# Second product of the opening feed-forwards as seven products of halves, with their late side panels on GpSimd

## The chip, the cores and the metric

One core of a Trainium2 chip runs the kernel. The metric is the device time of one execution in microseconds. The kernel before takes 2571.94 us (median of three runs, 2569.3 to 2572.46).

## The reference, cut to what matters

The kernel computes a first transformer block (mixers and a mixture of experts) and then a second one of two layers, all in fp32, for 256 tokens of width 1024. The change touches the first feed-forward of each of the two layers, and the modulation vector that is computed beside it:

```python
def swiglu(h, w_in, w_out):
    gate, up = jnp.split(h @ w_in, 2, axis=-1)
    return (jax.nn.silu(gate) * up) @ w_out
...
for l in range(DEPTH_2):
    mod = cond @ w_ada[l] + b_ada[l]
    sh1, sc1, g1, sh2, sc2, g2, sh3, sc3, g3 = jnp.split(mod, N_MOD, axis=-1)
    h = modulate_2(rms_norm_2(x), sh1, sc1)
    x = x + 0.5 * g1[:, None, :] * swiglu(h, w_ff1_in[l], w_ff1_out[l])
    ...
    h = modulate_2(rms_norm_2(x), sh3, sc3)
    x = x + 0.5 * g3[:, None, :] * swiglu(h, w_ff2_in[l], w_ff2_out[l])
```

The inner width of a feed-forward is 2816, which is 22 blocks of 128. The product in question is the one with `w_out`: 1024 x 2816 by 2816 x 256 tokens.

## The kernel before, in words

Activations lie transposed, features on the 128 partitions, 256 tokens along the free axis. The output of a feed-forward's second product is made in eight chunks of 128 features. Three stages matter: `first_layer`, `between` and `last`. `LayerIn` is the opening feed-forward of a layer with the projection behind it and runs in `first_layer` and in `between`; `LayerOut` is the closing feed-forward and runs in `between` and in `last`.

In both, the first product of the feed-forward is done in ten groups (`Groups`), each as seven products of halves (Strassen's scheme) instead of eight, with VectorE making the sums and differences of halves, and ScalarE taking results out of PSUM. A group takes TensorE about 12.5 us.

The second product differs. `LayerOut` uses `Down` (line 2022): two chunks of features form a pair, a pair and the two halves of the tokens form a 2x2 product of halves over 11 blocks, and each of the four pairs takes seven products of 11 matmuls with 128 columns. For each pair VectorE makes four differences of weights of 128x1408 (lines 2133 to 2149); once it makes five sums of halves of the hidden activations (line 2151), and for each pair it joins the products (`dve_join`, line 2162), updates the residual `xT` and scales the new chunk for what follows. `order` (line 2047) is the order of the products on TensorE, `made` (line 2049) the order in which VectorE finishes its results; each product waits for its count. `LayerIn` instead does plain products (`pe_add`, line 1796): 8 chunks of 22 matmuls with 256 columns, and `dve_add` behind each.

Beside the opening feed-forward runs the side work, the modulation vector `cond @ w_ada`. Its weights come in 28 side panels of 128x2048 through four side slots. `side_panel` (line 2622, VectorE) multiplies each half of a panel (1024 columns) by a per-partition factor and adds it to one of three totals; four panels make one tile of modulation values. Then TensorE sums the tile over the partitions (`tile_sum`, line 2308), ScalarE copies the row out, TensorE turns it (`turn`, line 2318) and VectorE adds the bias (`tile_add`, line 2616). Panels 0 to 15 lie beside the groups, panels 16 to 27 beside the chunks of the second product (`beside_chunk`, line 2227). SyncE loads the next panels when slots are free (`side_loads`, line 2272), in one queue with the feed-forward's weights and the weights of the projection that follows; `small` and `consts` are loaded once the last tile is summed, since `consts` holds the totals.

Behind the second product TensorE runs the leading product of the projection (`pe_lead`), which needs every scaled chunk and then one bank that the turns use. GpSimd does nothing in this stage; it clears two tiles later (line 2799).

Of the kernel before, what the change touches and what calls it, by code (L numbers as in the profile page):

```python
# [7 lines left out]
P = 128  # L8
D = 1024
KD = D // P  # L10
T = 256
# [7 lines left out]
KF = D_FF // P  # L19
# [1579 lines left out]
SIDE = 4  # L1599
GROUPS = 10  # L1600
# [421 lines left out]
class Down:  # L2022
# [3 lines left out]
    def __init__(self, st, c, d, l, ring, hid, room, scratch, tail, groups):  # L2026
        self.c, self.d, self.groups = c, d, groups
        self.made, self.product, self.kept = (st.sem(f"down{l}_{k}") for k in ("made", "product", "kept"))
# [11 lines left out]
        self.z = d.ps[5]  # L2040
# [38 lines left out]
    def pe_product(self, pe, p, i):  # L2079
# [22 lines left out]
        if p == 6:  # L2102
            self.wait_made(pe, f"t2_{i}")
            self.wait_made(pe, "s2")
            out, left, right = self.z[:, P:2 * P], self.t2, lambda k: self.s2[:, k]
# [7 lines left out]
        if p == 4:  # L2113
            self.wait_made(pe, f"t4_{i}")
            pe.wait_ge(self.kept, i + 1)
# [17 lines left out]
    def dve_weights(self, ve, i):  # L2133
# [28 lines left out]
    def dve_join(self, ve, i):  # L2162
        z, w, a, c = self.z, self.bank(i), self.a[i % 2], self.c
        ve.wait_ge(self.kept, i + 1)
        ve.wait_ge(self.product, self.count[3, i])
        if i:
            ve.wait_ge(self.d.x_updated, KD + 2 * i)
# [15 lines left out]
    def dve_odd(self, ve, i, gain):  # L2183
        d, q = self.d, 2 * i + 1
        ve.wait_ge(d.chunk_done, KD + 2 * i + 2)
# [5 lines left out]
class LayerIn:  # L2191
# [8 lines left out]
    def __init__(self, st, c, l, ring, buffers, ff_here, ps, xT, hT, cond, vec, small, mod, gain, proj, mix, consts, cst,  # L2200
                 tables, b, final_g, vec_src, small_src, consts_src, w_ada, w_ff, w_in, lead, begun, room, group_sems):
# [16 lines left out]
        groups = Groups(c, d, group_sems, l, hid, room, mix.rearrange("p k n -> p (k n)"))  # L2218
        x_sq = proj[:, 14:14 + KD]
# [111 lines left out]
        def tensor(pe, beside_values, beside_last):  # L2331
# [44 lines left out]
            d.pe_lead(pe, d.slots[0].rearrange("p (b n) -> p b n", n=P), 1, {3: lambda pe: d.pe_sum_folded(pe, 1)})\  # L2376
# [112 lines left out]
        def scalar(sc, beside_last):  # L2489
# [145 lines left out]

        def first_gain(ve):
# [4 lines left out]
        def vector(ve):  # L2641
# [1597 lines left out]
```

## Time and profile before

| | |
|---|---|
| median of three runs | 2571.94 us |
| the profiled execution's own time | 2572.24 us |
| its span, first to last instruction | 2570.5 us |
| TensorE busy (matmuls) | 2185.2 us, 85% |
| VectorE busy | 1118.7 us, 44% |
| ScalarE busy | 469.6 us, 18% |
| GpSimd busy | 6.1 us |
| mean granted TensorE clock | 0.933 |

PE is TensorE, PEld its weight loads, DVE is VectorE, ACT is ScalarE, POOL is GpSimd, SP is SyncE. A fp32 matmul stands in the trace as two records. A timeline row begins with the start and the length in us of a run of like instructions; the starts of successive rows show the pace, while the length of a row contains the pipeline's tail.

### The profile page before, as it was taken

How to read it: one execution, taken by the hardware profiler on the slowest of the kernel's cores; microseconds unless marked ns; L12 is line 12 of the kernel's file. 1: busy time of each engine (PE TensorE's matmuls, PEld its weight loads, DVE VectorE, ACT ScalarE, POOL GpSimd, SP SyncE). 2: the span in 40 equal slices, each digit the busy share in tenths (PEclk: the TensorE clock that was granted, in tenths of full speed). 3: DMA queues.
4: the chain of work that ended last, by engine and by line, in shares of the span. 5: the costliest groups of instructions: out<-in, count | busy, mean ns of one | idle time of the engine just before them, and what ended most of it. 6: DMA issues, size and time to landing. Idle time of an engine off the chain costs nothing. (4 is left out here: it accounts for less than half of the span.)

```text
span 2570.5 us, 30945 instructions
## 1 busy us (share of the span) xinstructions
PE 2185.2 (85%) x12430; PEld 1523.6 (59%) x12430; DVE 1118.7 (44%) x1941; ACT 469.6 (18%) x1049; POOL 6.1 (0%) x11
## 2 busy tenths in 40 slices
PE   8999986565666665655899999999999999999998
PEld 5786832111111211111588887788998888778898
DVE  5753631000000100000486557567668754756554
ACT  3204010000000000000222044322212203442220
POOL 0000000000000000000000000000000000000000
PEclk9999989878878788888999999999999999999999
DMA  9653799999999999999977632067447763115430
GB/s 391 231 223 122 282 411 416 428 428 428 428 428 427 428 428 428 428 427 427 420 305 290 256 106 84 2 274 299 165 197 289 278 258 141 49 49 215 173 153 17
DMA packets 75207, 721.61 MB, mean 281 GB/s; under 512 B 8656, under 2 KB 11728, under 8 KB 13520
## 3 DMA queue, kind: packets, MB, share of 16 engines
q1 hardware_dynamic: 75088, 719.95, 68.3%
q8 instruction: 83, 1.36, 0.2%
q14 instruction: 36, 0.29, 0.0%
HBM read 718.87 MB, written 1.05 MB: 280 GB/s over the span
## 5 line engine op out<-in xcount | busy, mean ns | idle before, releaser
L1315 PE MATMUL bank<-pool,moe_x_cur 128*32 128x512 f32 x1776 | 259.8, 722 | 143.1 <-DMA pool<-in_w_expert 143.1
L1315 PEld LDWEIGHTS bank<-pool,moe_x_cur 128*32 128x32 f32 x1776 | 54.2, 122 | 336.2 <-DMA pool<-in_w_expert 229.7
L1340 PE MATMUL bank<-pool,moe_hidT 128*32 128x512 f32 x864 | 148.0, 821 | 70.3 <-DMA pool<-in_w_expert 62.5
L1497 DVE TENSOR_TENSOR moe_hid<-bank,moe_silu 128x512 f32<-128x512 f32 x16 | 11.1, 691 | 443.4 <-ACT moe_silu L1457 443.4
L1809 PE MATMUL bank<-trunk_proj,pool 128*128 128x256 f32 x704 | 155.5, 380 | 0.0
L1887 PE MATMUL bank<-pool 128*128 128x256 f32 x640 | 152.1, 381 | 0.0
L1887 PE MATMUL bank<-spare,trunk_mix 128*128 128x256 f32 x640 | 146.7, 382 | 3.6 <-ACT first_layer_sq L1946 3.6
L2364 PE MATMUL bank<-pool 128*128 128x256 f32 x672 | 148.3, 380 | 0.0
L1887 PE MATMUL bank<-pool,trunk_mix 128*128 128x256 f32 x640 | 145.9, 381 | 0.0
L1809 PEld LDWEIGHTS bank<-trunk_proj,pool 128*128 128x128 f32 x704 | 132.5, 190 | 19.8 <-issue 2.5
L2364 PEld LDWEIGHTS bank<-pool 128*128 128x128 f32 x672 | 127.2, 190 | 21.2 <-issue 4.2
L1887 PEld LDWEIGHTS bank<-spare,trunk_mix 128*128 128x128 f32 x640 | 122.6, 192 | 20.9 <-issue 4.0
L1887 PEld LDWEIGHTS bank<-pool,trunk_mix 128*128 128x128 f32 x640 | 122.6, 192 | 17.0
L1340 PEld LDWEIGHTS bank<-pool,moe_hidT 128*32 128x32 f32 x864 | 28.2, 132 | 174.1 <-DMA pool<-in_w_expert 105.5
L1887 PEld LDWEIGHTS bank<-pool 128*128 128x128 f32 x640 | 117.6, 190 | 17.2 <-issue 3.3
L787 PE MATMUL bank<-pool 128*128 128x256 f32 x576 | 126.8, 379 | 1.0 <-PEq L3160 1.0
L1501 DVE COPY moe_y<-bank 128x512 f32<-128x512 f32 x16 | 11.1, 691 | 267.1 <-PE bank L1340 250.2
L787 PEld LDWEIGHTS bank<-pool 128*128 128x128 f32 x576 | 109.2, 190 | 19.1 <-issue 4.7
L1457 ACT ACTIVATE moe_silu<-bank 128x512 f32<-128x512 f32 x16 | 9.6, 597 | 564.6 <-PE bank L1315 564.6
L1354 PE MATMUL bank<-moe_place,moe_y 128*128 (+1 forms) x256 | 73.8, 439 | 43.8 <-DVE xT L1510 26.3
L1354 PEld LDWEIGHTS bank<-moe_place,moe_y 128*128 128x128 f32 x256 | 52.6, 216 | 78.7 <-DVE xT L1510 33.6
L1510 DVE SCALAR_TENSOR_TENSOR xT<-bank,first_mod,xT 128x256 f32<-128x256 f32 x128 | 53.2, 477 | 78.0 <-PE bank L1354 78.0
(689 smaller groups left out, 3202.8 us busy)
## 6 DMA issues: line engine op xcount, KB each, us to landing
pool<-in_w_expert SPq DMA_DIRECT2D x165, 2048.0 KB, 35.6
pool<-in_w_ff SPq DMA_DIRECT2D x132, 1024.0 KB, 6.9
pool<-in_w_ada SPq DMA_DIRECT2D x66, 1024.0 KB, 8.9
moe_more<-in_w_expert SPq DMA_DIRECT2D x23, 2048.0 KB, 36.1
pool<-in_w_in SPq DMA_DIRECT2D x40, 1024.0 KB, 4.9
pool<-in_w_mod SPq DMA_DIRECT2D x24, 1024.0 KB, 7.7
pool<-in_w_out SPq DMA_DIRECT2D x10, 1024.0 KB, 9.9
pool<-in_small SPq DMA_DIRECT2D x2, 2560.0 KB, 9.3
```

What stands on the lines that cost most here:

```text
L787: mm = pe.matmul(ps[p % 3][:, j * T:(j + 1) * T], w[:, j * KD + k], h[:, k], start=k == 0, stop=k == KD - 1)
L1315: mm = pe.matmul(ps[b][quarter[g], :], x_cur[:, u], w[:, b, g], start=u == 0, stop=u == up_panels - 1)
L1340: mm = pe.matmul(ps[2 + b][quarter[g], :], hidT[:, s, g], w[:, g, b], start=s == 0, stop=s == down_panels - 1)
L1354: mm = pe.matmul(ps[at][:, (j % 2) * T:(j % 2 + 1) * T], y[:, k * P:(k + 1) * P], place_of[:, e], start=True, stop=True)
L1457: sc.activation(silu, ps[0], ACT.Silu).then_inc(silu_done, 1)
L1497: ve.tensor_tensor(hid, ps[1], silu, MUL).then_inc(hid_done, 1)
L1501: ve.tensor_copy(y[:, 512:D], ps[3]).then_inc(y_high, 1)
L1510: m = ve.scalar_tensor_tensor(xT[:, k], ps[at][:, (j % 2) * T:(j % 2 + 1) * T], gate[:, k:k + 1], xT[:, k], MUL, ADD)
L1809: mm = pe.matmul(self.ps[3 + q % 2][:, 0:T], w, x[:, k], start=k == 0, stop=k == nk - 1)
L1887: mm = pe.matmul(bank, left[:, k], right[:, k], start=start and k == 0, stop=k == 3, skip_group_check=True)
L2364: mm = pe.matmul(ps[n % 3][:, j * T:(j + 1) * T], slot[:, j * KD + k], hT[:, k], start=k == 0, stop=k == KD - 1)
```

## The change

The second product of the opening feed-forwards goes through `Down` too. `Down` gets a base for its counts and the number of its PSUM bank. Its second difference of weights (`t2`) is written over the weights of the first product, which frees room, and so is a step of its own that waits for that product (`dve_second_weight`):

```diff
@@ -2023,21 +2023,20 @@
 
 
 
-    def __init__(self, st, c, d, l, ring, hid, room, scratch, tail, groups):
-        self.c, self.d, self.groups = c, d, groups
-        self.made, self.product, self.kept = (st.sem(f"down{l}_{k}") for k in ("made", "product", "kept"))
+    def __init__(self, d, sems, behind, ring, hid, room, scratch, tail, groups, z_bank, chunks_before):
+        self.d, self.groups, self.behind, self.base = d, groups, behind, chunks_before
+        self.made, self.product, self.kept = sems
         n = KH * P
         tall = lambda a: a.rearrange("p (k n) -> p k n", n=P)
         self.w = tall(ring[:, 0:KF * KD * P])
-        self.t1, self.t2 = tall(room[:, 0:n]), tall(room[:, n:2 * n])
-        self.s1, self.s2 = tall(scratch[:, 0:n]), tall(scratch[:, n:2 * n])
+        self.t1, self.s1, self.s2 = tall(room[:, 0:n]), tall(room[:, n:2 * n]), tall(scratch[:, 0:n])
         silu = d.silu.rearrange("p k n -> p (k n)")
-        self.s4_low, self.s4_last = tall(room[:, 2 * n:16 * T]), silu[:, 5 * P:6 * P]
+        self.s4_low, self.s4_last = tall(room[:, 2 * n:16 * T]), scratch[:, n:n + P]
         self.a = [silu[:, 2 * j * P:2 * (j + 1) * P] for j in range(2)]
         self.u2, self.c = silu[:, 4 * P:5 * P], tail
         self.a11, self.a21 = hid[:, 0:KH, 0:P], hid[:, 0:KH, P:T]
         self.a12, self.a22 = hid[:, KH:KF, 0:P], hid[:, KH:KF, P:T]
-        self.z = d.ps[5]
+        self.z = d.ps[z_bank]
         order = [(1, 0), (1, 1), (2, 0)]
         for i in range(PAIRS):
             order += [(5, i), (6, i), (7, i), (3, i)]
...
@@ -2049,14 +2048,14 @@
         made = ["t1_0", "t3_0", "t2_0", "s1", "s2", "s3", "s4_low", "s4_last", "t4_0"]
         for i in range(PAIRS):
             if i + 1 < PAIRS:
-                made += [f"{k}_{i + 1}" for k in ("t1", "t3", "t2")]
+                made += [f"{k}_{i + 1}" for k in ("t1", "t3")]
             made += [f"{k}_{i}" for k in ("u2", "c11", "u3", "u4", "c22", "c12")]
             if i + 1 < PAIRS:
-                made += [f"t4_{i + 1}"]
+                made += [f"{k}_{i + 1}" for k in ("t2", "t4")]
             made += [f"c21_{i}"]
-        self.made_at = {k: n + 1 for n, k in enumerate(made)}
+        self.made_at = {k: len(made) * behind + n + 1 for n, k in enumerate(made)}
         self.order = order
-        self.count = {p: n + 1 for n, p in enumerate(p for p in order if p[0] != 4)}
+        self.count = {p: 6 * PAIRS * behind + n + 1 for n, p in enumerate(p for p in order if p[0] != 4)}
 
     def weights(self, i):
         low = lambda q: self.w[:, q * KF:q * KF + KH]
...
@@ -2137,16 +2136,18 @@
             ve.wait_ge(self.product, self.count[5, i - 1])
         ve.tensor_tensor(self.t1, b12, b11, SUB).then_inc(self.made, 1)
         ve.tensor_tensor(b12, b22, b12, SUB).then_inc(self.made, 1)
+
+    def dve_second_weight(self, ve, i):
+        b11, _, _, b22 = self.weights(i)
         self.wait_made(ve, f"t1_{i}")
-        if i:
-            ve.wait_ge(self.product, self.count[6, i - 1])
-        ve.tensor_tensor(self.t2, b22, self.t1, SUB).then_inc(self.made, 1)
+        ve.wait_ge(self.product, self.count[1, i])
+        ve.tensor_tensor(b11, b22, self.t1, SUB).then_inc(self.made, 1)
 
     def dve_last_weight(self, ve, i):
-        _, _, b21, _ = self.weights(i)
+        t2, _, b21, _ = self.weights(i)
         ve.wait_ge(self.product, self.count[2, i])
         self.wait_made(ve, f"t2_{i}")
-        ve.tensor_tensor(b21, b21, self.t2, SUB).then_inc(self.made, 1)
+        ve.tensor_tensor(b21, b21, t2, SUB).then_inc(self.made, 1)
 
     def dve_halves(self, ve):
         g = self.groups
```

In `pe_product` the sixth product reads `b11` in place of `self.t2`; counts in `dve_join`, `act_keep` and `dve_odd` get the base; `LayerOut` calls `dve_second_weight` where the third difference was. In `LayerIn` the loops over chunks are replaced on TensorE and ScalarE:

```diff
@@ -2216,6 +2217,7 @@
         side_slots = [ring[:, at + u * BLK * P:at + (u + 1) * BLK * P] for u in range(SIDE)]
         hid = proj[:, 0:KF]
         groups = Groups(c, d, group_sems, l, hid, room, mix.rearrange("p k n -> p (k n)"))
+        down = Down(d, down_sems, l, ring, hid, room, hT.rearrange("p k n -> p (k n)"), proj[:, KF:KF + 2], groups, 2, 0)
         x_sq = proj[:, 14:14 + KD]
         inverse = inverse_of(room)
 
...
@@ -2344,13 +2346,19 @@
                     tile_sum(pe, n_early + sum_behind[g])
                 if g in turn_behind:
                     turn(pe, n_early + turn_behind[g])
-            for q in range(KD):
-                d.pe_add(pe, q, hid, KF, 0, d.panels(), d, 1, ready=groups.ready)
-
-                if q in sum_chunk:
-                    tile_sum(pe, n_early + sum_chunk[q])
-                if q in turn_chunk:
-                    turn(pe, n_early + turn_chunk[q])
+            for p, i in down.order:
+                if (p, i) == (4, PAIRS - 1):
+                    turn(pe, n_early + 5)
+                    tile_sum(pe, n_early + 6)
+                down.pe_product(pe, p, i)
+                if (p, i) == (1, 0):
+                    groups.pe_turn(pe, GROUPS - 1)
+                if p == 4:
+                    if 0 < i < PAIRS - 1:
+                        turn(pe, n_early + 2 + i)
+                    if i < PAIRS - 1:
+                        tile_sum(pe, n_early + 3 + i)
+            turn(pe, n_early + 6)
 
             def in_pair(n):
                 slot = d.slots[n % 4].rearrange("p (b n) -> p b n", n=P)
...
@@ -2373,7 +2381,8 @@
                 mm.then_inc(l_summed, 1)
 
             pe.wait_ge(d.loaded[0], in_before[0] + 16)
-            d.pe_lead(pe, d.slots[0].rearrange("p (b n) -> p b n", n=P), 1, {3: lambda pe: d.pe_sum_folded(pe, 1)})\
+            d.pe_lead(pe, d.slots[0].rearrange("p (b n) -> p b n", n=P), 1,
+                      {3: lambda pe: d.pe_sum_folded(pe, 1), KD - 1: lambda pe: pe.wait_ge(added, n_early + 7)})\
                 .then_inc(in_done, 1)
             in_pair(1)
             in_pair(2)
...
@@ -2505,10 +2514,16 @@
             groups.act_out(sc, GROUPS - 1)
 
             sc.activation(hb[:, 0, :, 0], c["eps"][:, 0:NT], ACT.Sqrt)
-            for q in range(KD):
-                d.act_added(sc, q, 0, 1)
-                if q in sum_chunk:
-                    tile_rows(sc, n_early + sum_chunk[q])
+            down.act_keep(sc, 0)
+            for i in range(PAIRS):
+                if i + 1 < PAIRS:
+                    down.act_keep(sc, i + 1)
+                else:
+                    tile_rows(sc, n_early + 6)
+                for q in (2 * i, 2 * i + 1):
+                    d.act_added(sc, q, 0, 1)
+                if i + 1 < PAIRS:
+                    tile_rows(sc, n_early + 3 + i)
             d.act_norm(sc, 1, mod[:, 24:32], 1)
 
             def pair_out(n):
```

and on VectorE, whose panels 16 to 27 go to GpSimd:

```diff
@@ -2633,6 +2648,27 @@
             ve.wait_ge(acc_step, r + 1)
             ve.scalar_tensor_tensor(total, w[:, 1], cond[:, 2 * j + 1, 2:3], total, MUL, ADD).then_inc(side_done, 1)
 
+        def side_panel_beside(pool, n):
+            r = early + n
+            tile, j = divmod(order_of(r), 4)
+            total, step = acc[:, tile % 3], early + 16 + 2 * (n - 16) - (n - 16 + 3) // 4
+            w = side_slots[r % SIDE].rearrange("p (k n) -> p k n", k=2)
+            pool.wait_ge(side_loaded[r % SIDE], 16 * (r // SIDE + 1))
+            pool.wait_ge(side_done, r)
+            if j == 0:
+
+                pool.wait_ge(sums_made, (tile if early else tile - 2) - 2)
+            first = total if j == 0 else w[:, 0]
+            pool.tensor_scalar(first, w[:, 0], cond[:, 2 * j, 2:3], None, MUL)
+            pool.tensor_scalar(w[:, 1], w[:, 1], cond[:, 2 * j + 1, 2:3], None, MUL).then_inc(acc_step, 1)
+            pool.wait_ge(acc_step, step + 1)
+            if j == 0:
+                pool.tensor_tensor(total, total, w[:, 1], ADD).then_inc(side_done, 1)
+            else:
+                pool.tensor_tensor(w[:, 1], w[:, 0], w[:, 1], ADD).then_inc(acc_step, 1)
+                pool.wait_ge(acc_step, step + 2)
+                pool.tensor_tensor(total, total, w[:, 1], ADD).then_inc(side_done, 1)
+
         def first_gain(ve):
             link = Chain(ve, chain)
             ve.wait_ge(added, 2)
...
@@ -2680,12 +2716,31 @@
             d.dve_lead_shift(ve, mod[:, 24:32])
             ve.tensor_scalar(gain[:, 1], mod[:, 32:40], 1.0, None, ADD)
             link(ve.tensor_scalar(gain[:, 3], mod[:, 16:24], 0.5, None, MUL))
-            for q in range(KD):
-                for n in beside_chunk[q]:
-                    side_panel(ve, early + n)
-                d.dve_add(ve, q, 0, gain[:, 3], d, 1, gain[:, 1])
-                if q in turn_chunk:
-                    tile_add(ve, n_early + turn_chunk[q])
+            down.dve_weights(ve, 0)
+            down.dve_second_weight(ve, 0)
+            down.dve_halves(ve)
+            down.dve_last_weight(ve, 0)
+            for i in range(PAIRS):
+                if i + 1 < PAIRS:
+                    down.dve_weights(ve, i + 1)
+                down.dve_join(ve, i)
+                down.dve_even(ve, i, gain[:, 3])
+                if i + 1 < PAIRS:
+                    down.dve_second_weight(ve, i + 1)
+                    down.dve_last_weight(ve, i + 1)
+                else:
+                    tile_add(ve, n_early + 5)
+                if i:
+                    d.dve_fold(ve, 1, 2 * i - 1)
+                    d.dve_fold(ve, 1, 2 * i)
+                ve.wait_ge(d.x_updated, 2 * i + 1)
+                d.dve_lead(ve, 2 * i, gain[:, 1])
+                down.dve_odd(ve, i, gain[:, 3])
+                ve.wait_ge(d.x_updated, 2 * i + 2)
+                d.dve_lead(ve, 2 * i + 1, gain[:, 1])
+                if 0 < i < PAIRS - 1:
+                    tile_add(ve, n_early + 2 + i)
+            tile_add(ve, n_early + 6)
             ve.wait_ge(added, n_early + 7)
             ve.tensor_scalar(gain[:, 2], mod[:, 56:64], 1.0, None, ADD)
             ve.tensor_scalar(gain[:, 4], mod[:, 64:72], 0.5, None, MUL)
...
@@ -2797,6 +2852,8 @@
             ve.tensor_tensor(rope, rope, b["turned"], ADD).then_inc(q_ready, 1)
 
         def gpsimd(pool):
+            for n in range(16, rest):
+                side_panel_beside(pool, n)
 
             pool.wait_ge(prepared, 1)
             pool.memset(x_blocks, 0.0).then_inc(cleared, 1)
```

The three semaphores of `Down` are made once for a stage and handed in. The loads on SyncE keep their lines.

## Rows read from the trace of the kernel before

**Rows 1.** The page: busy time of each engine, TensorE's slices and its granted clock.

```profile
PE 2185.2 (85%) x12430; PEld 1523.6 (59%) x12430; DVE 1118.7 (44%) x1941; ACT 469.6 (18%) x1049; POOL 6.1 (0%) x11
...
PE   8999986565666665655899999999999999999998
...
PEclk9999989878878788888999999999999999999999
```

**Rows 2.** Timeline of TensorE, first layer: start us, us, line, op, count.

```profile
1404.14 3.62 PE L1809 MATMUL bank<-trunk_proj,pool 128*128 128x256 f32 x16
...
1414.17 0.64 PE L2314 MATMUL bank<-trunk_consts,ones 128*32 128x256 f32 x8
1414.73 9.76 PE L1809 MATMUL bank<-trunk_proj,pool 128*128 128x256 f32 x44
...
1425.27 9.66 PE L1809 MATMUL bank<-trunk_proj,pool 128*128 128x256 f32 x44
1434.77 0.38 PE L2324 MATMUL bank<-ident,first_layer_rows 128*128 128x128 f32 x2
1434.99 9.66 PE L1809 MATMUL bank<-trunk_proj,pool 128*128 128x256 f32 x44
...
1484.45 1.90 PE L1733 MATMUL bank<-trunk_mix,pool 128*128 128x257 f32 x8
...
1506.08 0.59 PE L2382 MATMUL bank<-trunk_proj,trunk_consts 128*128 128x256 f32 x2
```

**Rows 3.** Timeline of TensorE, second layer.

```profile
2054.54 3.62 PE L1809 MATMUL bank<-trunk_proj,pool 128*128 128x256 f32 x16
...
2134.85 1.90 PE L1733 MATMUL bank<-trunk_mix,pool 128*128 128x257 f32 x8
```

**Rows 4.** Timeline of TensorE in the closing feed-forward of the first layer.

```profile
1842.81 2.62 PE L2118 MATMUL bank<-trunk_proj,pool 128*128 128x128 f32 x22
1845.27 0.60 PE L1928 MATMUL bank<-ident,spare 128*128 128x128 f32 x4
...
1857.99 2.40 PE L2118 MATMUL bank<-spare,pool 128*128 128x128 f32 x20
...
1912.04 1.90 PE L1733 MATMUL bank<-trunk_mix,pool 128*128 128x257 f32 x8
```

**Rows 5.** VectorE by line, 1400 to 1490 us: count, then busy us, mean ns.

```profile
L2634 DVE SCALAR_TENSOR_TENSOR trunk_consts<-pool,cond,trunk_consts 128x1024 f32<-128x1024 f32 x12 | 15.4, 1285 | 0.4
...
L2628 DVE TENSOR_SCALAR trunk_consts<-pool,cond 128x1024 f32<-128x1024 f32 x3 | 2.2, 748 | 0.0
```

**Rows 6.** VectorE by line in the closing feed-forward, 1842.8 to 1914 us.

```profile
L2138 DVE TENSOR_TENSOR spare<-pool 128x1408 f32<-128x1408 f32 x4 | 6.5, 1624 | 2.5 <-PE bank L2118 2.5
...
L1725 DVE TENSOR_SCALAR trunk_mix<-xT,gain 128x256 f32<-128x256 f32 x8 | 2.8, 351 | 0.1
...
L2181 DVE SCALAR_TENSOR_TENSOR xT<-trunk_proj,gain,xT 128x256 f32<-128x256 f32 x4 | 1.9, 484 | 0.1
```

**Rows 7.** Timeline of VectorE, same feed-forward: start us, us.

```profile
1844.06 1.63 DVE L2138 TENSOR_TENSOR spare<-pool 128x1408 f32<-128x1408 f32 x1
1845.61 1.62 DVE L2139 TENSOR_TENSOR pool<-pool 128x1408 f32<-128x1408 f32 x1
...
1854.81 0.28 DVE L2160 TENSOR_TENSOR between_silu<-trunk_proj,trunk_consts 128x128 f32<-128x128 f32 x1
```

**Rows 8.** Timeline of VectorE, last group of the first layer's opening feed-forward.

```profile
1394.45 1.28 DVE L2634 SCALAR_TENSOR_TENSOR trunk_consts<-pool,cond,trunk_consts 128x1024 f32<-128x1024 f32 x1
...
1400.86 0.43 DVE L2007 TENSOR_TENSOR spare<-first_layer_sq 128x256 f32<-128x256 f32 x1 [1.72 <-ACT first_layer_sq L1946]
```

**Rows 9.** GpSimd by line, whole span.

```profile
L2802 POOL MEMSET pool<- 128x1024 f32 x2 | 1.9, 953 | 2191.1 <-DVE pool L2761 2191.1
```

**Rows 10.** DMA issues, 1390 to 1530 us: count, KB, median us to landing.

```profile
pool<-in_w_ada SPq DMA_DIRECT2D x10, 1024.0 KB, 7.4
...
trunk_consts<-table_mixer_consts SPq DMA_DIRECT2D x1, 1920.0 KB, 13.5
```

More of the change, by code:

```diff
@@ L2104, in pe_product @@
             self.wait_made(pe, "s2")
-            out, left, right = self.z[:, P:2 * P], self.t2, lambda k: self.s2[:, k]
+            out, left, right = self.z[:, P:2 * P], b11, lambda k: self.s2[:, k]
         if p == 7:
@@ L2114, in pe_product @@
             self.wait_made(pe, f"t4_{i}")
-            pe.wait_ge(self.kept, i + 1)
+            pe.wait_ge(self.kept, PAIRS * self.behind + i + 1)
             out, left, right = self.bank(i)[:, 2 * P:3 * P], b21, lambda k: self.a22[:, k]
@@ L2163, in dve_join @@
         z, w, a, c = self.z, self.bank(i), self.a[i % 2], self.c
-        ve.wait_ge(self.kept, i + 1)
+        ve.wait_ge(self.kept, PAIRS * self.behind + i + 1)
         ve.wait_ge(self.product, self.count[3, i])
         if i:
-            ve.wait_ge(self.d.x_updated, KD + 2 * i)
+            ve.wait_ge(self.d.x_updated, self.base + 2 * i)
         ve.tensor_tensor(self.u2, z[:, P:2 * P], a[:, 0:P], ADD).then_inc(self.made, 1)
@@ L2200, in __init__ @@
     def __init__(self, st, c, l, ring, buffers, ff_here, ps, xT, hT, cond, vec, small, mod, gain, proj, mix, consts, cst,
-                 tables, b, final_g, vec_src, small_src, consts_src, w_ada, w_ff, w_in, lead, begun, room, group_sems):
+                 tables, b, final_g, vec_src, small_src, consts_src, w_ada, w_ff, w_in, lead, begun, room, group_sems, down_sems):
         d = self.d = Dense(st, c, ring, ps, xT, hT, f"in{l}", buffers, ff_here, 96 * l, l)
@@ L2817, with __init__ @@
 class LayerOut:
-    def __init__(self, st, c, l, ring, buffers, ff_here, ps, xT, hT, mod, gain, mix, hid, out_slots, w_ff, after, lead, room, group_sems, scratch,
-                 tail):
+    def __init__(self, st, c, l, ring, buffers, ff_here, ps, xT, hT, mod, gain, mix, hid, out_slots, w_ff, after, lead, room, group_sems, down_sems,
+                 scratch, tail):
         d = self.d = Dense(st, c, ring, ps, xT, hT, f"out{l}", buffers, ff_here, 48 + 96 * l, l + 1, False)
@@ L2830, in __init__ @@
         groups = Groups(c, d, group_sems, 0, hid, room, mix.rearrange("p k n -> p (k n)"))
-        down = Down(st, c, d, l, ring, hid, room, scratch, tail, groups)
+        down = Down(d, down_sems, 0, ring, hid, room, scratch, tail, groups, 5, KD)
         def sync(sp):
@@ L2941, in vector @@
             down.dve_weights(ve, 0)
+            down.dve_second_weight(ve, 0)
             down.dve_halves(ve)
@@ L2949, in vector @@
                 if i + 1 < PAIRS:
+                    down.dve_second_weight(ve, i + 1)
                     down.dve_last_weight(ve, i + 1)
@@ L4077, in second_block, with down_sems, layer_in, layer_out @@
         cs = unpack(consts, "mixer_consts")
+        def down_sems(st):
+            return [st.sem("down_" + k) for k in ("made", "product", "kept")]
         def group_sems(st):
             return [st.sem("group_" + k) for k in ("combined", "product", "taken", "joined", "silued", "turned", "hid_out")]
-        def layer_in(st, l, buffers, sems):
+        def layer_in(st, l, buffers, sems, downs):
             return LayerIn(st, c, l, ring, buffers, ff_here, ps, xT, hT, cond, vec, small, mod, gain, proj, mix, consts, cs,
                            tables, b, v1("final_g"), I["vec2"][l], I["small2"][l], cst["mixer_consts"], I["w_ada"][l],
-                           I["w_ff1"][l], I["w_in_2"][l], lead_in, first_lead(pool), room, sems)
-        def layer_out(st, l, buffers, after, sems):
+                           I["w_ff1"][l], I["w_in_2"][l], lead_in, first_lead(pool), room, sems, downs)
+        def layer_out(st, l, buffers, after, sems, downs):
             return LayerOut(st, c, l, ring, buffers, ff_here, ps, xT, hT, mod, gain, mix, proj[:, 0:KF], w_out_slots,
-                            I["w_ff2"][l], after, lead_out, room, sems, consts, proj[:, KF:KF + 2])
+                            I["w_ff2"][l], after, lead_out, room, sems, downs, consts, proj[:, KF:KF + 2])
         w_out_here = [tr.sem(f"w_out_here{u}") for u in range(SIDE)]
@@ L4097, in second_block @@
         with Stage(nc, "first_layer") as st:
-            enter = layer_in(st, 0, dense_buffers(st), group_sems(st))
+            enter = layer_in(st, 0, dense_buffers(st), group_sems(st), down_sems(st))
             mixed = mixers(st, 0, enter)
@@ L4126, in second_block @@
             buffers = dense_buffers(st)
-            sems = group_sems(st)
-            enter = layer_in(st, 1, buffers, sems)
-            leave = layer_out(st, 0, buffers, enter, sems)
+            sems, downs = group_sems(st), down_sems(st)
+            enter = layer_in(st, 1, buffers, sems, downs)
+            leave = layer_out(st, 0, buffers, enter, sems, downs)
             mixed = mixers(st, 1, enter)
@@ L4163, in second_block @@
                           mix.rearrange("p k n -> p (k n)").rearrange("p (t h d) -> p t h d", t=NT, h=2), out)
-            leave = layer_out(st, 1, buffers, store, group_sems(st))
+            leave = layer_out(st, 1, buffers, store, group_sems(st), down_sems(st))
             with st.block() as block:
```

2 lines of the change are left out of this document (1 added, 1 removed).

## The prediction

> **What bounds the kernel now.** I read the page's busy shares first, then TensorE's timeline around the two opening feed-forwards, then VectorE's and GpSimd's groups. TensorE is busy 85% of the span, VectorE 44%, GpSimd 6.1 us in all; from the second half on TensorE's slices are at 9 tenths and its granted clock too [rows 1]. So TensorE sets the time wherever it isn't waiting, and the stage that is changed is one of those places: from 1404.14 to 1484.45, 80.31 us, the second product runs without a gap [rows 2], and the page's granted clock is 9 tenths or more there [rows 1], the 2.4 GHz level; 128x256 records at 0.216 us apart are that pace [rows 2]. The second layer's stage has the same length, 2054.54 to 2134.85 [rows 3]. The reader is to see there that 44 records (22 matmuls, each recorded twice) take 9.50 us between starts, and that four side sums of 0.56 us, four side turns of about 0.22 us and one turn of 0.44 us lie between them.
>
> **TensorE's part.** The same seven-product form already runs in the closing feed-forwards: 22 records of 128x128 by 128 columns in 2.46 us between starts, the whole of 28 products and one turn of 0.44 us from 1842.81 to 1912.04, 69.23 us, without a wait [rows 4]. The changed stage would be 28 x 2.456 = 68.8, + 0.44, + 4 sums x 0.56, + 4 turns x 0.22 = 72.4 us. Against 80.3 that is 7.9 us less for each layer, 15.9 in all. Behind the last product nothing is late by itself: in the closing stage the join after its third product, its last updates and the scaled chunks come in time for the matmuls that follow at 1912.04 [rows 4], and the join here is the same. What is new is the wait ahead of the second half of the leading product for the last modulation column; its turn stands 16 short matmuls earlier and its add takes 0.16 us, so I give it 0, at most 1 us.
>
> **VectorE's part.** Twelve panels go: 21 steps of 1.285 and 3 x 0.748 = 29.2 us [rows 5]. Added are 16 differences of weights at 1.62 [rows 6], five sums of halves (three of 1408 elements, one of 1280, one of 128: 6.6 us), four joins (six of 0.28 each, as any 128x128 form [rows 7]). In the closing stage that load (45 us of 69) stands beside TensorE and is just in time: the first halves' sums end at 1855.1, TensorE wants the last of them at 1857.99 [rows 4, 7]. At the opening of the stage there are 3 us of cover at most, and nothing in the middle is closer. Left alone, it costs nothing.
>
> **GpSimd's part, the term that decides.** It takes 12 panels of each layer: in nine of them two scalings and two adds, in three (the first of a modulation tile) two scalings and one add, all 128x1024 fp32. That is 24 scalings and 21 adds. It can start when VectorE has ended panel 15 at 1395.73 [rows 8] and must have ended before the last side sum, which now stands ahead of the last product: 1404.14 + 27 x 2.456 + 0.44 + 3 x 0.56 + 3 x 0.22 = 1473.2. It has 77.5 us. The earlier sums want four and eight panels by about 1445 and 1462; they are looser.
>
> The trace has no GpSimd arithmetic. Nearest is its memset of 128x1024, 0.953 us [rows 9]. Bounds: a scaling reads one stream while it writes one, from 0.95 (reading hidden) to 1.9 (one after the other). An add has three streams: from 0.95 to 2.9. VectorE's own ratio of two-input to one-input work (1.285 to 0.748) would give 1.6. I take 0.95 for the scaling and 2.3 for the add (two reads one after the other, the write partly beside them; between 1.9 and 2.9). Sum: 24 x 0.95 + 21 x 2.3 = 71.1 us. What its hand-overs between dependent instructions cost no row shows; on VectorE the successor of a dependent step starts within hundredths of a us, so I leave it at nothing here and 3 us at most. So 71 of 77.5 us: it just fits, if nothing else holds it.
>
> Beside that, the Trainium skill ("GPSIMD Engine Reference", section 3.1) has 4497 ns for an add of 2048 fp32 elements, so some 2.25 us here as an estimate; no run here shows it yet. By it alone the sum is 1 us shorter.
>
> What can hold it is VectorE, which streams SBUF beside it. No row shows both at once. Bounds: nothing, and all of it one after the other. VectorE's instructions with both inputs in SBUF, or with the one-input form that runs at 0.73 ns per element (twice the pace, so it plainly moves two elements at a time), are in this stretch: 16 differences 26.0 us, halves 6.6, eight chunk updates 3.9, eight scaled chunks 2.8 [rows 6], one add of each join 1.1 [rows 7], six folds and three adds of the last group, 128x256 at 0.43, 3.9 [rows 8]. That is 44.3; less 2.8 for those of the last pair, which come after GpSimd's end, and less 0.08 for each of some 40 (they start 1.54 apart and last 1.62 [rows 7]) it is 38 us. One after the other, GpSimd ends 71.1 + 38 = 109 us after 1395.73, 31.5 late. The stage then lasts 72.4 + 31.5 = 103.9 us, 23.6 more than before.
>
> I take the full exclusion, since either price is extreme and even two fifths of it lose: 6.4 us of slack and 7.9 us of gain are used up by 14 us of 38. The Trainium skill speaks against the change here ("SBUF — State Buffer", section "Who interferes with whom"): a VectorE instruction with two SBUF inputs and a GpSimd one that reads SBUF block each other for a whole instruction. The trace can't show it; by it GpSimd is late as above, without it the change gains.
>
> Exclusion also holds VectorE: GpSimd's mean instruction is 71.1 / 45 = 1.6 us, and before each of the nine opening instructions VectorE would wait for one, some 14 us against 3 us of cover [rows 7]. TensorE then stands waiting for sums of halves and weights. This runs beside GpSimd's lateness, and is not added: both end at about the same time.
>
> **DMAs and queues.** SyncE's side loads wait for panels (two ahead of each of the first four w_in loads). The loads of panels 20 to 27 are let go by panels 16 to 23, and each lands 7.4 us after issue against 6.4 or more for a panel on GpSimd with four slots: hidden. The loads of small and of the constants follow the last side sum; the later lands 13.5 us after issue [rows 10]. TensorE wants them at 1506.08, now 24 us behind the last side sum (last product 2.5, leading product 7.8, two pairs 13.8) [rows 2]: hidden with 10 us to spare. GpSimd's memsets of the next stage wait for VectorE far later; GpSimd is free long before.
>
> **Sum.** The profiled execution took 2572.24 us (span 2570.5 and 1.7 around it), 0.3 above the median of the runs, 2571.94. 2572.24 + 2 x 23.6 = 2619.4; I say 2619.
>
> **The rivals.**
> Both engines stream side by side. GpSimd ends after some 71 us, before it is wanted, and the whole 15.9 us are gained: 2556. For it: PSUM-fed joins and TensorE don't touch GpSimd, and the fit of 71 in 77 us holds. Against it: GpSimd's own sum keeps that fit only while an add stays under 2.6 us. It decides faster from slower at 85.4 us of GpSimd time after 1395.73.
> GpSimd alone is too slow: scalings at 1.6 and adds at 3.0 make 101 us, 24 late, 16 more per layer: 2604. Nothing in the rows is as slow; its memset speaks against it.
> The exclusion, and TensorE's clock falls in the waits. Where TensorE was busy 5 or 6 tenths, the granted clock was 7 or 8 tenths [rows 1]. The 24 us of matmuls behind the last side sum at 0.8 take 6 us more for each layer: 2631.
> The exclusion is only partial (two fifths): both signs meet near 2572.
>
> **How the numbers follow.** The exclusion 0.50, with the clock 0.07, GpSimd alone slow 0.09; side by side 0.30; partial 0.04. What this measurement can tell from no change is 0.2%, 5 us. So faster 0.30, same 0.04, slower 0.66. Cases of both signs hold much of the chance, so the range reaches from the gaining case, 2553 (15.9 gained and 3 for the small gaps between the rows that I rounded), to exclusion with adds at 2.9 us: 21 x 0.6 = 12.6 us later per layer, 2645. The likeliest case by itself: 2590 (adds at 1.6: 14.7 earlier per layer) to 2645.
>
> **What would show it.** Right: GpSimd's adds at 2 us or more in the trace; VectorE's 1408-element differences, 1.62 us before, longer or started late while GpSimd runs; the last side sum waiting tens of us for the tile of sums; the stage near 104 us with TensorE waiting. Wrong: differences still 1.62 us beside a running GpSimd, the last side sum without a wait, the stage near 72 us. TensorE's 22 records should take 2.46 us in either case.

## The result and the profile after

The changed kernel takes 2684.32 us (median of four runs, 2681.69 to 2686.03), the kernel before 2570.62 beside it: ratio 1.0444, 95% interval 1.0432 to 1.0457. It is 114 us slower; I had said 2619, with a range up to 2645. The sign was right and the size was not.

The page of the changed kernel: TensorE does the same 2185.2 us of work, GpSimd 279.9 us in place of 6.1 [rows 1], and there are two dents in TensorE's row of slices.

```profile
PE 2185.2 (82%) x12958; PEld 1535.5 (57%) x12958; DVE 1188.1 (44%) x1991; ACT 472.9 (18%) x1057; POOL 279.9 (10%) x101
...
PE   8999887566666656567998399999999955999998
...
PEclk9999997788778888878999699999999977999999
```

The dents are the two changed stages. TensorE's timeline in the first layer, which answers to [rows 2], is to be read by the waits in brackets:

```profile
1401.33 2.62 PE L2117 MATMUL bank<-trunk_proj,pool 128*128 128x128 f32 x22
...
1410.26 2.69 PE L2117 MATMUL bank<-spare 128*128 128x128 f32 x22 [0.96 <-DVE spare L2155]
1413.95 2.69 PE L2117 MATMUL bank<-pool 128*128 128x128 f32 x22 [0.99 <-DVE pool L2157]
1417.63 2.69 PE L2117 MATMUL bank<-trunk_proj,pool 128*128 128x128 f32 x22 [0.99 <-DVE trunk_proj L2158]
...
1445.49 0.38 PE L2326 MATMUL bank<-ident,first_layer_rows 128*128 128x128 f32 x2
1449.27 1.08 PE L2316 MATMUL bank<-trunk_consts,ones 128*32 128x256 f32 x8 [3.40 <-POOL trunk_consts L2670]
...
1468.65 0.38 PE L2326 MATMUL bank<-ident,first_layer_rows 128*128 128x128 f32 x2
1493.06 1.08 PE L2316 MATMUL bank<-trunk_consts,ones 128*32 128x256 f32 x8 [24.02 <-POOL trunk_consts L2670]
...
1505.34 0.38 PE L2326 MATMUL bank<-ident,first_layer_rows 128*128 128x128 f32 x2
1533.58 1.08 PE L2316 MATMUL bank<-trunk_consts,ones 128*32 128x256 f32 x8 [27.85 <-POOL trunk_consts L2670]
1534.59 4.28 PE L2117 MATMUL bank<-trunk_proj,pool 128*128 128x128 f32 x22
...
1538.92 1.90 PE L1733 MATMUL bank<-trunk_mix,pool 128*128 128x257 f32 x8
```

From 1401.33 to 1538.92 is 137.59 us against 80.31 before. The three sums and differences at the opening wait about 1 us each; the sums of tiles 4, 5 and 6 wait 3.40, 24.02 and 27.85 us for GpSimd's last add of their tile. The records that follow a long wait are slow ones: 22 in 4.1 us (1534.59 to 1538.70, granted clock 0.60 there) against 2.46; from 1538.92 on the granted clock is 1.00 again. One stretch, with the mean granted clock in third place from the end, answers to TensorE's busy 80.31 of 80.31 us before:

```profile
1401.33:1538.92 137.59, 79.36 (x661) 75.29 (x660) 72.09 (x77) 7.90 (x19) 128.73 (x42) 0.80 0.32 123
```

The second layer's stage lasts 137.9 us (2107.55 to 2245.41), so the two stages make 57.3 + 57.6 = 114.9 us. The rest of the kernel is unchanged within 3 us of each stretch. The question is only why GpSimd ended 140.5 us after its start (1392.93, panel 15's end, to 1533.43) where I had 109.

GpSimd by line, to read beside [rows 9] (both layers together; count, then busy us and mean ns):

```profile
L2663 POOL TENSOR_SCALAR pool<-pool,cond 128x1024 f32<-128x1024 f32 x24 | 81.2, 3384 | 0.0
L2662 POOL TENSOR_SCALAR pool<-pool,cond 128x1024 f32<-128x1024 f32 x18 | 58.6, 3254 | 3.1 <-POOL trunk_consts L2670 2.0 <-POOL trunk_consts L2666 1.0
L2670 POOL TENSOR_TENSOR trunk_consts<-trunk_consts,pool 128x1024 f32<-128x1024 f32 x18 | 52.4, 2910 | 1.4
L2668 POOL TENSOR_TENSOR pool<-pool 128x1024 f32<-128x1024 f32 x18 | 49.6, 2756 | 1.5
L2662 POOL TENSOR_SCALAR trunk_consts<-pool,cond 128x1024 f32<-128x1024 f32 x6 | 17.1, 2847 | 1890.0 <-DVE trunk_consts L2649 1889.4 <-issue 0.6
L2666 POOL TENSOR_TENSOR trunk_consts<-trunk_consts,pool 128x1024 f32<-128x1024 f32 x6 | 15.4, 2574 | 0.5
```

and in order of time, first layer, while VectorE is busy (up to 1474) and when it is idle (1482 and later):

```profile
1393.12 2.85 POOL L2662 TENSOR_SCALAR trunk_consts<-pool,cond 128x1024 f32<-128x1024 f32 x1 [1392.08 <-DVE trunk_consts L2649]
...
1404.21 4.62 POOL L2663 TENSOR_SCALAR pool<-pool,cond 128x1024 f32<-128x1024 f32 x1
1408.92 3.40 POOL L2668 TENSOR_TENSOR pool<-pool 128x1024 f32<-128x1024 f32 x1
1412.40 3.61 POOL L2670 TENSOR_TENSOR trunk_consts<-trunk_consts,pool 128x1024 f32<-128x1024 f32 x1
1416.18 5.34 POOL L2662 TENSOR_SCALAR pool<-pool,cond 128x1024 f32<-128x1024 f32 x1 [0.17 <-POOL trunk_consts L2670]
1421.50 5.67 POOL L2663 TENSOR_SCALAR pool<-pool,cond 128x1024 f32<-128x1024 f32 x1
...
1482.41 2.84 POOL L2662 TENSOR_SCALAR pool<-pool,cond 128x1024 f32<-128x1024 f32 x1 [0.17 <-POOL trunk_consts L2670]
...
1488.15 2.34 POOL L2668 TENSOR_TENSOR pool<-pool 128x1024 f32<-128x1024 f32 x1
...
1531.09 2.34 POOL L2670 TENSOR_TENSOR trunk_consts<-trunk_consts,pool 128x1024 f32<-128x1024 f32 x1
```

Alone, a scaling of 128x1024 takes 2.85 us and an add 2.34. Beside VectorE a scaling takes up to 5.67 and an add up to 3.61. Busy time for one layer is 274.3 / 2 = 137.2 us; alone the same 45 instructions would take 24 x 2.85 + 21 x 2.34 = 117.5. So 19.6 us of it is stretching beside VectorE, and 3.1 us lie between instructions.

VectorE's side of the same moments (a 1408-element sum was 1.62 us before [rows 6]):

```profile
1406.12 2.46 DVE L2144 TENSOR_TENSOR pool<-pool,spare 128x1408 f32<-128x1408 f32 x1
1408.50 1.61 DVE L2155 TENSOR_TENSOR spare<-trunk_proj 128x1408 f32<-128x1408 f32 x1
1410.15 3.65 DVE L2157 TENSOR_TENSOR pool<-spare,trunk_proj 128x1408 f32<-128x1408 f32 x1
1413.72 3.76 DVE L2158 TENSOR_TENSOR trunk_proj<-trunk_proj 128x1408 f32<-128x1408 f32 x1
1417.41 1.48 DVE L2160 TENSOR_TENSOR spare<-trunk_proj,pool 128x1280 f32<-128x1280 f32 x1
1418.81 1.12 DVE L2161 TENSOR_TENSOR pool<-trunk_proj,pool 128x128 f32<-128x128 f32 x1
```

The sum at 1408.50 started ahead of GpSimd's add and keeps its 1.61 us, and the add is stretched to 3.40; those at 1410.15 and 1413.72, beside GpSimd's two adds, take 3.65 and 3.76; the next, beside a scaling that is itself stretched to 5.34, is short again. A scaling isn't free for VectorE either: the difference at 1406.12 takes 2.46 in place of 1.62 beside the scaling of 1404.21, and the 128x128 sum at 1418.81 takes 1.12 in place of 0.28 [rows 7], 0.84 us more each. That is far less than beside an add.

### The profile page after: what moved, and what is told of

The parts are those of the page before. It is cut to its first block and busy times, and to the rows that moved or that the text cites. A ratio compares the mean times of both kernels' runs of the same rounds, so it can differ in the third digit from the quotient of the medians.

```text
span 2681.0 us, 32252 instructions
## 1 busy us (share of the span) xinstructions
PE 2185.2 (82%) x12958; PEld 1535.5 (57%) x12958; DVE 1188.1 (44%) x1991; ACT 472.9 (18%) x1057; POOL 279.9 (10%) x101
## 5 line engine op out<-in xcount | busy, mean ns | idle before, releaser
L1315 PE MATMUL bank<-pool,moe_x_cur 128*32 128x512 f32 x1776 | 268.8, 741 | 147.3 <-DMA pool<-in_w_expert 147.3
L2662 POOL TENSOR_SCALAR trunk_consts<-pool,cond 128x1024 f32<-128x1024 f32 x6 | 17.1, 2847 | 1890.0 <-DVE trunk_consts L2649 1889.4
L2117 PE MATMUL bank<-trunk_proj,pool 128*128 128x128 f32 x1408 | 167.3, 278 | 2.0 <-DVE trunk_proj L2158 2.0
L2117 PEld LDWEIGHTS bank<-trunk_proj,pool 128*128 128x128 f32 x1408 | 163.8, 195 | 4.1 <-DVE trunk_proj L2158 2.3
L2316 PE MATMUL bank<-trunk_consts,ones 128*32 128x256 f32 x128 | 12.7, 476 | 110.5 <-POOL trunk_consts L2670 110.5
```

Source lines behind the costliest of these rows:

```text
L1315: mm = pe.matmul(ps[b][quarter[g], :], x_cur[:, u], w[:, b, g], start=u == 0, stop=u == up_panels - 1)
L2117: mm = pe.matmul(out, left[:, k], right(k), start=k == 0, stop=k == KH - 1)
L2316: mm = pe.matmul(ps[5][32 * g:32 * g + 32, 0:2 * P], c["ones"][:, 0:32], acc[:, tile_of(n) % 3, g * 2 * P:(g + 1) * 2 * P], start=True, st ...
L2662: pool.tensor_scalar(first, w[:, 0], cond[:, 2 * j, 2:3], None, MUL)
```

## The experiments

Ratios are to the kernel before, run beside them.

**Only the arithmetic of GpSimd left out.**

```diff
-            pool.tensor_scalar(first, w[:, 0], cond[:, 2 * j, 2:3], None, MUL)
-            pool.tensor_scalar(w[:, 1], ...).then_inc(acc_step, 1)
...
+            pool.sem_inc(side_done, 1)
```

> The changed kernel with GpSimd's arithmetic on panels 16 to 27 left out (it only counts them as done), so the late modulation values are not computed; everything else as changed. Theory (GpSimd's work is the whole loss, the seven products and VectorE's part are sound): the stage falls from 137.6 us to about 72.4, and the time to 2555 +- 3, that is 15.9 under the kernel before. Rival (VectorE's added differences and sums, or the new order of turns and sums, hold TensorE on their own): stage above 76 us, time 2562 or more.

Measured: 2555.47 us, ratio 0.9944 (0.9928 to 0.9961); the stage lasts 73.15 us (1405.63 to 1478.78), with no wait of TensorE in it. By the medians it is 12.8 us faster than the kernel beside it (2568.3). The seven products, VectorE's added 45 us and the new order are sound, as the theory had it: the whole loss is GpSimd's.

**The plain second product with GpSimd's panels.** The other half of the change alone.

```diff
-                for n in beside_chunk[q]:
-                    side_panel(ve, early + n)
+        def gpsimd(pool):
+            for n in range(16, rest):
+                side_panel_beside(pool, n)
-        sum_chunk, turn_chunk = {0: 3, 1: 4, 3: 5, 5: 6}, {1: 3, 2: 4, 4: 5, 6: 6}
+        sum_chunk, turn_chunk = {0: 3, 3: 4, 5: 5, 6: 6}, {1: 3, 4: 4, 6: 5, 7: 6}
```

> The kernel before with its plain second product, and only panels 16 to 27 handed to GpSimd (the last sums and turns of tiles moved behind later chunks). GpSimd's own work by the durations now seen alone, 24 scalings x 2.85 + 21 adds x 2.34 = 117.5 us, + 45 small gaps of 0.08 and 12 of 0.1 (5 us), from 1395.7 on, so the last side sum at about 1519 against 1476. Theory A (GpSimd's own speed makes most of the loss, exclusion little): each stage 45 to 50 us longer, time 2660 to 2672. Theory B, the one I predicted by (exclusion with the 16 differences of weights makes the loss): those differences are gone here, so GpSimd is nearly in time and the time is below 2610.

Measured: 2663.08 us, ratio 1.0361 (1.0342 to 1.0379). Its scalings take 2.84 to 2.93 us in the mean and its adds 2.34 to 2.35, 118.5 us for a layer: nearly no exclusion, and nearly the whole loss. The theory that I had predicted by falls: exclusion with the differences of weights isn't what makes GpSimd late in the main. Its own speed is. It isn't all of the loss, though: GpSimd's work costs 94.8 us here (2663.1 against 2568.3) and 128.8 us beside the seven products (2684.3 against 2555.5), so about a quarter comes with VectorE's two-input work.

**The scalings on ScalarE, the adds on GpSimd.**

```diff
+            sc.activation(w[:, 0], w[:, 0], ACT.Copy, scale=cond[:, 2 * j, 2:3]).then_inc(acc_step, 1)
+            sc.activation(w[:, 1], w[:, 1], ACT.Copy, scale=cond[:, 2 * j + 1, 2:3]).then_inc(acc_step, 1)
...
-            pool.tensor_scalar(first, w[:, 0], cond[:, 2 * j, 2:3], None, MUL)
-            pool.tensor_scalar(w[:, 1], w[:, 1], cond[:, 2 * j + 1, 2:3], None, MUL).then_inc(acc_step, 1)
```

> The changed kernel with the 24 scalings of a layer moved from GpSimd to ScalarE (which is busy 8 of 138 us there); the 21 adds stay on GpSimd. Theory A (the scalings, 2.85 us each where I wrote 0.95, are what is over): GpSimd has 49 us + waits + exclusion on its adds (about 1 us each, 20) = some 75 us of 77: the last wait of 27.9 us shrinks to under 8, and the time is 2556 to 2575. Theory B (exclusion is the greater part, and an add suffers as much as a scaling): GpSimd ends 30 us or more late in each layer, time above 2610.

Measured: 2592.45 us, ratio 1.0096 (1.0079 to 1.0114), between the two. Nearly four fifths of the loss is gone (24 us over the kernel beside it, where the change had 114): the scalings on GpSimd were most of it. Theory A had the last wait right (1.5 us) but not what the adds do to VectorE. A scaling takes ScalarE 1.14 us. The stage is 92.7 us (1399.49 to 1492.17), with waits of TensorE of 1.4, 4.0, 6.8 and 1.5 us, three of them for VectorE. The timeline of VectorE shows why, at the second pair:

```profile
1417.62 3.77 DVE L2137 TENSOR_TENSOR spare<-pool 128x1408 f32<-128x1408 f32 x1
1421.32 3.77 DVE L2138 TENSOR_TENSOR pool<-pool 128x1408 f32<-128x1408 f32 x1
1425.01 0.28 DVE L2169 TENSOR_TENSOR first_layer_silu<-bank,first_layer_silu 128x128 f32<-128x128 f32 x1
1425.21 2.22 DVE L2170 TENSOR_TENSOR trunk_proj<-first_layer_silu 128x128 f32<-128x128 f32 x1
```

Two differences at 3.77 in place of 1.62 and a 128x128 add at 2.22 in place of 0.28 delay the join that frees the bank; TensorE waits 3.95 us for it. The 22 records behind the waits of 4.0 and 1.5 us are slow as well, 4.8 and 4.6 us at granted clocks of 0.50 and 0.53. In this kernel the exclusion and the clock behind its waits, not GpSimd's lateness, are most of what is left.

**The late panels on VectorE, in the gaps of the seven-product form.**

```diff
+                for n in ((), (18,), (22,), (26, 27))[i]:       # ahead of the join
+                    side_panel(ve, early + n)
+                for n in ((), (19,), (23,), ())[i]:             # behind the last difference
+                for n in ((16, 17), (20, 21), (24, 25), ())[i]: # at the end of the pair
```

> The changed kernel with panels 16 to 27 on VectorE as before, put into the gaps between its steps of the seven-product form. VectorE then has 45 us (joins, weights, halves) + 29.2 us of panels = 74 us for a stage of 72.4, starting with 9 steps that can't be late. Theory A: it is over by a few us only: stage 76 to 82, time 2560 to 2574, about the kernel before or a little under. Theory B (the in-order queue of VectorE makes each panel a wait for TensorE): stage above 88, time above 2585.

Measured: 2567.71 us, ratio 0.9993 (0.9983 to 1.0002): stage 78.4 us, three waits for sums of tiles of 1.65, 1.83 and 1.53 us. Theory A holds; there is no gain that can be told from none.

**GpSimd that only writes.**

```diff
...
+            for n_round in range(3):
+                pool.memset(w[:, 0], 0.0)
+                m = pool.memset(w[:, 1], 0.0)
```

> The changed kernel with GpSimd's arithmetic on a late panel replaced by six memsets of 128x1024 that only write (0.95 us each, 68 us for a layer, the late modulation values not computed). Theory A (the exclusion is over SBUF reads: two-input VectorE work against GpSimd work that reads): VectorE's 1408-element differences stay at 1.62 us and no GpSimd memset is longer than 0.96; stage 72 to 75, time 2554 to 2560. Theory B (any two instructions of the two engines exclude each other): differences 2.2 us or more in the mean, memsets lengthened by up to 1.6 us, GpSimd at about 100 us, stage above 95.

Measured: 2556.58 us, ratio 0.9949 (0.9930 to 0.9967); the 144 memsets took 0.955 to 0.957 us in the mean. VectorE by line, 1405 to 1465 us:

```profile
L2150 DVE TENSOR_TENSOR pool<-pool 128x1408 f32<-128x1408 f32 x4 | 6.5, 1624 | 1.6 <-PE bank L2117 1.5
...
L1725 DVE TENSOR_SCALAR trunk_mix<-xT,gain 128x256 f32<-128x256 f32 x6 | 5.4, 898 | 0.1
```

The differences keep 1.62 us, so two-input work isn't held by a GpSimd that only writes. The one-input chunk scalings (L1725) are: 0.90 us in the mean against 0.35 [rows 6]. Theory A holds for two-input work and is too narrow for the quick one-input form. It costs TensorE nothing here.

**A constant in place of the factor per partition.**

```diff
-            pool.tensor_scalar(first, w[:, 0], cond[:, 2 * j, 2:3], None, MUL)
+            pool.tensor_scalar(first, w[:, 0], 0.5, None, MUL)
```

> The changed kernel with the scalings on GpSimd multiplied by a constant in place of the per-partition factor read from SBUF (the late modulation values are wrong by that). Theory A (the 2.85 us of a scaling is the form with a factor per partition): the scaling falls to 1.0 to 1.6 us, GpSimd's work by 30 to 44 us for a layer, time 2595 to 2625. Theory B (a one-input instruction costs GpSimd 2.85 whatever its factor): time 2684 +- 5 as the changed kernel.

Measured: 2664.70 us, ratio 1.0369 (1.0350 to 1.0388). Alone a scaling takes 2.77 us, not 2.85: the factor per partition costs 0.08. So the price is of the one-input form. The time is still 20 us under the changed kernel, which neither theory had: GpSimd's busy time per layer is 127.6 us, 12.0 over the sum of the lone durations where the changed kernel has 19.6. So the same two kinds of instruction, each scaling 0.08 us shorter, cost 7.6 us a layer less in exclusion. That this comes from which instructions happen to meet is my reading; no run tests it.

**The scaling as a two-input product.**

```diff
+            by = lambda k: cond[:, k, 2:3].broadcast_to([P, 1024])
+            pool.tensor_tensor(first, w[:, 0], by(2 * j), MUL)
```

> The changed kernel with each scaling on GpSimd written as a two-input product, its second input the factor's column repeated by a step of zero. Theory A (GpSimd's two-input form is the quicker one, 2.34 against 2.85 us alone, though it reads more): 24 x 0.5 = 12 us less for a layer, time 2655 to 2665. Theory B (a repeated column is read at its own slower pace, or the exclusion grows with the second input): no less than 2680.

Measured: 2652.79 us, ratio 1.0323 (1.0304 to 1.0342), a gain a little beyond theory A's. GpSimd alone, the product and the add:

```profile
1391.11 1.89 POOL L2663 TENSOR_TENSOR trunk_consts<-pool,cond 128x1024 f32<-128x1024 f32 x1 [1390.07 <-DVE trunk_consts L2649]
...
1394.93 2.35 POOL L2667 TENSOR_TENSOR trunk_consts<-trunk_consts,pool 128x1024 f32<-128x1024 f32 x1
```

1.89 us where the one-input form has 2.85, an add of two full inputs 2.35. It still loses, and now for another reason:

```profile
1418.04 5.03 PE L2117 MATMUL bank<-spare 128*128 128x128 f32 x22 [10.71 <-DVE spare L2155]
...
1515.66 0.66 PE L2326 MATMUL bank<-ident,first_layer_rows 128*128 128x128 f32 x2 [6.86 <-DVE mod L2635]
1516.25 1.08 PE L2316 MATMUL bank<-trunk_consts,ones 128*32 128x256 f32 x8
```

TensorE never waits for GpSimd in this stage of the first layer (1399.36 to 1520.78, 121.4 us); all its waits, 35.4 us, are for VectorE. Beside GpSimd's two-input products VectorE's 1408-element differences and sums take mostly 3.1 to 3.8 us in place of 1.62. What the quicker form saves on GpSimd's lateness, most of it comes back as exclusion on VectorE.

**Four panels only on GpSimd**, eight on VectorE.

```diff
-            for n in range(16, rest):
+            for n in range(16, 20):
                 side_panel_beside(pool, n)
```

> The changed kernel with four late panels (16 to 19) on GpSimd and the other eight on VectorE in the gaps of the seven-product form. GpSimd's four panels need 8 x 2.85 + 7 x 2.34 = 39 us alone and are wanted some 51 us after they can start, so lateness is out and only the exclusion is left. Theory A (exclusion costs TensorE what it cost at the opening of the changed kernel, 2.9 us there, and up to 3.4 us at the sum behind the second pair, little elsewhere): stage 76 to 80, time 2563 to 2571. Theory B (without lateness GpSimd's help is free): stage under 74, time 2554 to 2558.

Measured: 2583.23 us, ratio 1.0043 (1.0028 to 1.0059), worse than either theory had. GpSimd needed 55.1 us for its 15 instructions where the lone durations give 39.2. TensorE waited 2.9 us at the opening, 3.4 for GpSimd's tile and 1.6 twice for VectorE, and its records after the 3.4 us were slow (22 in 4.85 us, granted clock 0.50). The stage is 86.6 us. Even in a small dose GpSimd's help costs more than VectorE's own panels do (78.4 us with all twelve on VectorE).

**All panels on VectorE, most of them earlier.** VectorE has room beside the ten groups, so two panels go beside each.

```diff
-        beside_group = [(2,), (3, 4), (5,), (6, 7), (8,), (9, 10), (11,), (12, 13), (14,), (15,)]
+        beside_group = [(2 * g + 2, 2 * g + 3) for g in range(GROUPS)]
-        sum_behind, turn_behind = {2: 0, 4: 1, 7: 2}, {3: 0, 5: 1, 8: 2}
+        sum_behind, turn_behind = {2: 0, 3: 1, 5: 2, 7: 3, 9: 4}, {3: 0, 4: 1, 6: 2, 8: 3}
+                for n in ((), (22,), (24, 25), (26, 27))[i]:   # ahead of the join; 23 behind it
```

> The changed kernel with all side panels on VectorE again, two beside each of the ten groups (panels 2 to 21) and only six (22 to 27) in gaps of the seven-product form; sums and turns of tiles follow them. Theory: VectorE has 4.6 + 1.7 + 5.2 = 11.5 us of work in a group of 12.5 and 45 + 15 = 60 us in a stage of 72.4, so it keeps up and the whole gain of the seven products is had: stage 72 to 74, time 2553 to 2558, ratio 0.994 to 0.996, both kernels beaten. Rival: VectorE's queue, now 92% full beside the groups, or SyncE's loads that wait for panels, hold TensorE there: each group 1 us or more longer, 20 us in all, time 2570 or more.

Measured: 2559.22 us, ratio 0.9961 (0.9947 to 0.9975). Faster than both kernels, less than hoped. One wait is left in each layer, at the first sum of halves:

```profile
1410.96 2.69 PE L2117 MATMUL bank<-spare 128*128 128x128 f32 x22 [1.47 <-DVE spare L2155]
```

The next kernel moves panel 21 from behind the last group into the second pair (`+ [(20,)]` as the last entry, `(21, 22)` ahead of that pair's join):

> e5_earlier_on_vector with one panel moved from behind the last group (where its two steps, 2.6 us, stood ahead of the first differences of weights and made TensorE wait 1.47 us for the first sum of halves) into the second pair of the seven-product form. Theory (that wait is VectorE's queue and nothing else): it goes in both layers, 2.9 us, time 2555 to 2557, ratio 0.9945 to 0.9955. Rival (a later panel makes a new wait of the same size at the sum of tile 5 or in the second pair): 2558 to 2560, no change from e5.

Measured: 2555.22 us, ratio 0.9944 (0.9931 to 0.9958). The intervals of this kernel and the one ahead of it overlap, so the step between them is shown by the trace and not by the times. The wait is gone and no new one has come; the first sum starts right behind the product ahead of it:

```profile
1401.61 2.72 PE L2117 MATMUL bank<-trunk_proj,pool 128*128 128x128 f32 x22
...
1409.51 2.62 PE L2117 MATMUL bank<-spare 128*128 128x128 f32 x22
...
1473.11 1.90 PE L1733 MATMUL bank<-trunk_mix,pool 128*128 128x257 f32 x8
```

The stage is 71.5 us, two sums of tiles having moved into the groups. This is the version to keep: 15.3 us faster than the kernel before, 129 us faster than the change.

## Why the prediction was wrong, point by point

- **TensorE's part, 72.4 us and 15.9 us gained: right.** 73.15 us without GpSimd's work, 12.8 us gained by the medians; 15.9 lies in the interval of the ratio.
- **VectorE's part costs nothing left alone: right.** The stage without late panels has no wait of TensorE.
- **A scaling at 0.95 us: the step that failed.** It measured 2.85, three times my value and half as much again as my upper bound of 1.9. 24 x 1.9 = 45.6 us more for a layer. I took the memset's pace for a form that also reads, and took for the upper bound "one stream after the other"; neither gave what the instruction takes. I also assumed that one input is cheaper than two: it is dearer here (2.85 against 2.34). The rival "GpSimd alone is too slow" was the right mechanism, with 0.09, and it too had the scaling at 1.6.
- **An add at 2.3 us: right**, 2.34 (0.8 us more a layer). The Trainium skill's figure ("GPSIMD Engine Reference", section 3.1), 2.25 as an estimate from it, agrees. The same page's selection table (section 4.1) calls one-input work "roughly line-rate", by which a scaling would take some 0.85 us as an estimate (1024 elements, one for each cycle of the 1.2 GHz that section 3.1 works with); the rows have 2.85, and the measurement decides.
- **Hand-overs at nothing: 3.1 us** a layer, my bound.
- **Exclusion, 38 us: the mechanism is real, the size was 19.6.** It is not total, and for the last two fifths of the time VectorE had next to nothing to do (5.0 us from 1474 to 1533.43), because TensorE stood waiting. The Trainium skill ("SBUF — State Buffer", section "Who interferes with whom") has an exclusive lock held for a whole instruction. The adds agree: 3.6 us for GpSimd's and 3.77 for VectorE's. The scalings don't agree: one is stretched to as much as 5.7 us while most of VectorE's instructions pass it at 1.6, and single ones beside it are 0.6 to 0.8 us longer.
- **VectorE late by 14 us at the opening: wrong**, 2.9 us of waits, since VectorE is held by the adds and passes the scalings nearly unhindered. With the scalings as two-input products the waits at the opening were 10.7 and 2.2 us, near what I had.
- **The tail and the clock:** 5.5 us from GpSimd's end to the leading product, where I had 3.2; the product behind the last wait ran at the slow pace (4.1 us for 2.46). A rival had put the clock at 6 us a layer, too much.
- **DMAs hidden: right.** Neither GpSimd's panels nor TensorE behind the stage waited for a load.

The sum: GpSimd's end moved by 45.6 + 0.8 + 3.1 - 18.4 = 31.1 us, the tail by 2.3, 33.4 of the 33.7 us by which a stage is longer than predicted (137.6 against 103.9). The two mistakes in opposite directions would have hidden each other in the total had they been of a size; the run with the plain second product takes them apart. The chances followed the same picture: the upper end of the range held an add at 2.9 but never together with a dearer scaling.

## What to carry to other kernels

An engine whose arithmetic isn't in the trace has no price: measure each form of its instruction once before its load is planned to 92% of a window, and don't let a memset stand for it. Before work goes to an idle but slow engine that shares something with the busy one, look for room on the busy one in an earlier stage: with five of the twelve late panels moved ahead beside the groups and seven left in the stage, all on VectorE, the kernel gained all that GpSimd was meant to give. Where two costs are uncertain, the range must contain each one's bound together, not one at a time.

## What the runs showed of the hardware that was not expected

- GpSimd, 128x1024 fp32, alone: one-input scaling 2.85 us (2.77 with a constant), two-input add 2.34, product with a repeated column 1.89, memset 0.95.
- A GpSimd add and a VectorE two-input instruction hold each other for most of the other's length (3.6 us for 2.34 and 3.77 for 1.62). Beside a GpSimd one-input scaling VectorE's mostly keep their 1.6 us, with 0.6 to 0.8 us more on single ones, and the scaling stretches to 5.7.
- The product with a repeated column is quicker alone, but holds VectorE as an add does: 1408-element instructions of 3.1 to 3.8 us beside it, and TensorE waited 35.4 us for VectorE in the first layer.
- A GpSimd that only writes leaves two-input VectorE work alone, but the quick one-input form goes from 0.35 to 0.90 us in the mean.
- TensorE's records after waits of 24 and 28 us, and after one of 3.4 us that followed other waits, were slow at first: 22 in 3.6 to 4.9 us against 2.46, at granted clocks of 0.69 to 0.50, the last of them the 1.2 GHz level.
